# Gated delta rule on one core: key and query products built once per token block and kept in SBUF, and an output projection from seven block products

## The reference, cut to what matters

```python
q = l2norm(...) * GDN_DK ** -0.5; k = l2norm(...); v = ...     # 8 heads of 128
o_fwd = chunk_gated_delta(q, k, v, beta[:, :, 0], g[:, :, 0])
o_bwd = flip(chunk_gated_delta(flip(q), flip(k), flip(v), flip(beta[:, :, 1]), flip(g[:, :, 1])))
o = rmsnorm(o_fwd + o_bwd, norm_g) * silu(z)
return o.reshape(B, S, H * GDN_DV) @ w_out                     # [512, 1024] @ [1024, 1024]
...
L = where(strict, (kb @ k.T) * decay, 0);  T = inverse(eye + L)
u = T @ vb;  w = T @ (kb * exp(gc));  a_intra = (q @ k.T) * decay
v_new = u - w @ state;  o = (q * exp(gc)) @ state + a_intra @ v_new
state = state * g_last + kg.T @ v_new
```

## Time and profile before

| | us |
|---|---|
| runs | 1690.05, 1692.55, 1693.95; median 1692.55 |
| the profiled execution | 1698.45 |
| its span | 1696.7 |
| TensorE busy | 1596.5 |
| GDN periods 0 to 4 | 921.2 to about 1106.5 |
| output projection | 1106.5 to 1164.4 |

### The profile page before, as it was taken

One profiled execution on the slowest core, in us unless ns is written; L12 is line 12 of the kernel. 1 busy time (PEld: TensorE's weight loads), 2 busy tenths in 40 slices (PEclk: granted clock), 3 DMA queues, 4 the chain that ended last, 5 costly groups with the idle time before them and its releaser, 6 DMA issues.

```text
span 1696.7 us, 21245 instructions
## 1 busy us (share of the span) xinstructions
PE 1596.5 (94%) x8966; PEld 823.3 (49%) x8966; DVE 648.9 (38%) x1107; ACT 439.8 (26%) x972; POOL 183.1 (11%) x115
## 2 busy tenths in 40 slices
PE   7999899999989978899999999998999999999787
PEld 4464534343343324488875688855344433433233
DVE  3564411131210116789982566633111312102056
ACT  4232301101101003422125775542111010110043
POOL 2302000000000004352402211000000000000021
PEclk9999999999999999999999999999999999999999
DMA  8104699999999995012121110284899999999941
GB/s 289 72 14 185 267 422 424 396 427 430 425 426 425 428 424 202 0 50 101 50 100 50 27 27 2 101 347 198 369 426 391 428 426 428 424 428 428 426 184 50
DMA packets 54045, 454.56 MB, mean 268 GB/s; under 512 B 5187, under 2 KB 7519, under 8 KB 28991
## 3 DMA queue, kind: packets, MB, share of 16 engines
q1 hardware_dynamic: 53424, 452.90, 65.0%
q0 software_dynamic: 288, 0.22, 0.0%
q10 hardware_dynamic: 239, 0.09, 0.0%
HBM read 451.07 MB, written 2.13 MB: 267 GB/s over the span
## 4 chain that ended last, share of the span: by engine, by line
PE 70%; DMA 12%; DVE 11%; ACT 6%; issue 2%; DVEq 0%; ACTq 0%
PE banks L2116 31%; PE banks L1464 10%; DMA ring<-in_moe_w_down 8%; DVE misc L2540 4%; PE banks L2087 3%; PE banks L1745 3%; PE banks L1647 3%; PE banks L1999 3%; DMA ring<-in_moe_w_up 3%; PE banks L2149 3%; PE banks L1710 2%; PE banks L2177 2%; PE banks L1572 1%; PE banks L2125 1%; DVE misc L2538 1%
## 5 line engine op out<-in xcount | busy, mean ns | idle before, releaser
L2116 PE MATMUL banks<-ring,misc 128*64 128x512 f32 x1984 | 444.7, 599 | 10.7 <-DMA ring<-in_moe_w_up 5.7
L2116 PEld LDWEIGHTS banks<-ring,misc 128*64 128x64 f32 x1984 | 139.2, 138 | 286.8 <-issue 266.5
L2116 PE MATMUL banks<-ring,hid_t 128*64 128x512 f32 x960 | 216.1, 602 | 15.6 <-DMA ring<-in_moe_w_down 15.6
L2939 DVE TENSOR_TENSOR work<-work,banks 128x512 f32<-128x512 f32 x32 | 33.7, 1053 | 442.0 <-PE banks L2116 442.0
L1403 ACT ACTIVATE misc<-banks 32x512 f32<-32x512 f32 x64 | 37.5, 586 | 416.9 <-PE banks L2116 416.5
L2116 PEld LDWEIGHTS banks<-ring,hid_t 128*64 128x64 f32 x960 | 69.1, 138 | 153.0 <-issue 144.3
L2954 DVE COPY misc<-banks 32x512 f32<-32x512 f32 x64 | 44.2, 691 | 229.7 <-PE banks L2116 229.2
L798 POOL TENSOR_TENSOR ring<-ring 128x2048 f32<-128x2048 f32 x2 | 10.9, 5454 | 1098.2 <-DVE ring L2990 1098.2
L1464 PE MATMUL banks<-ring,xt 128*128 128x512 f32 (+1 forms) x280 | 118.9, 584 | 0.2
L2540 DVE SCALAR_TENSOR_TENSOR misc<-ring,conv_w,misc 128x512 f32<-128x512 f32 x96 | 93.8, 977 | 3.4
L1647 PE MATMUL banks<-ring 128*128 128x256 f32 x384 | 86.0, 380 | 0.0
(11 more groups left out here) (381 smaller groups left out, 1899.0 us busy)
## 6 DMA issues: line engine op xcount, KB each, us to landing
ring<-in_moe_w_gate SPq DMA_DIRECT2D x62, 2048.0 KB, 15.4
ring<-in_moe_w_up SPq DMA_DIRECT2D x62, 2048.0 KB, 18.3
ring<-in_moe_w_down SPq DMA_DIRECT2D x56, 2048.0 KB, 19.9
ring<-in_gdn_w_in SPq DMA_DIRECT2D x8, 2048.0 KB, 9.0
ring<-in_ple_w_gate SPq DMA_DIRECT2D x4, 2048.0 KB, 16.5
ring<-in_moe_w_down SPq DMA_DIRECT2D x6, 1024.0 KB, 23.6
ring<-in_mla_w_out SPq DMA_DIRECT2D x2, 2048.0 KB, 23.9
misc<-in_moe_w_down SPq DMA_DIRECT2D x2, 2048.0 KB, 15.7
```

The source lines that it names most:

```text
L2116: mm = pe.matmul(psum[64 * f:64 * f + 64, bank, :], tokens(4 * kh + k), row(k, f), start=(kh == 0 and k == 0), stop=(kh == 1 and k == 3))
```

## The change

Builds. `build_kk` runs for problems 0 and 2 only, `build_qk` likewise, into new stages `kb` and `qb` of 8 instead of 16 builds each, which ScalarE copies to SBUF (`keep_kk`, `keep_qk`). DVE reads the copies. They lie in `h`, which is written to DRAM before and read back after. Places: `keep_kk(0, a)` before the first exponentials; `kb` 0 to 3 as before; `qb` 0 to 3 at the end of period 0; `kb` 4 to 7 between the joins of period 1; `qb` 4 to 7 between those of period 2. The first product with the state (`new_state` or `with_state("qs")`, lane 0) moves to just after `dt5`.

Projection. Seven products of half the depth (`P1` to `P7`, two token blocks each) replace eight outputs of full depth. DVE makes two token sums and changes `a12`, GpSimd makes four weight sums and one token sum; DVE adds 28 times instead of 8.

```diff
+GO_PARTS = P1, P7, P2, P6, P5, P3, P4
+GO_ADDS = {P1: ((0, 0), (0, 1), (1, 0), (1, 1)), P7: ((1, 0), (1, 1)), P2: ((0, 0),), P6: ((0, 1), (1, 0), (1, 1)),
+           P5: ((0, 1), (1, 1)), P3: ((0, 1),), P4: ((1, 0),)}
...
-                if q + 1 < QS:
+                if q == 1:
                     for a in range(4):
-                        build_banks.add(core["kk"], 4 * q + 4 + a)
-                for a in range(4):
-                    build_banks.add(core["qk"], 4 * q + a)
+                        build_banks.add(core["kb"], 4 + a)
+                if q % 2 == 0:
+                    for a in range(4):
+                        build_banks.add(core["qb"], 2 * q + a)
...
                     for name in ("z5", "du5", "dt5", "z6"):
+                        if name == "z6" and p >= 2:
+                            apply_banks.add(core["st" if p % 2 == 0 else "qs"], 4 * (p // 2 - 1))
                         apply_banks.add(core[name], p - 1)
...
# SyncE
+                        if u == 2:
+                            sp.wait_ge(ple_added, 8)
+                            sp.dma_start(h_dram, flat_h).then_inc(x_in[3], 16)
...
                     sp.dma_start(gw_out[0], wo[:, :, 0:HALF]).then_inc(loaded[2], 16)
+                    for name in ("kk", "qk"):
+                        core[name].wait_read(sp, 15)
+                    sp.dma_start(flat_h, h_dram).then_inc(x_in[3], 16)
...
-                    frees[2] = s_go.full(8)
-                for m in ((0, 1, 2, 3, 6, 7, 4, 5), (1, 2, 3, 4, 6, 7, 0, 5))[l]:
+                    frees[2] = s_go.full(14)
+                    frees[7] = s_go.full(10)
+                for m in ((0, 1, 2, 3, 6, 7, 4, 5), (1, 3, 4, 6, 7, 0, 2, 5))[l]:
                     sp.wait_ge(*frees[slot_of(l, m)])
+                    if l == 1 and m == 2:
+                        sp.wait_ge(mo_weights, 8 + 5)
...
# GpSimd
+                wait_use(pool, "gdn_out0")
+                pool.wait_ge(gdn_out1_in, 16)
+                pool.wait_ge(*core["av"].full(12))
+                pool.tensor_tensor(go_t1, go_b12, go_b11, ALU.subtract).then_inc(mo_weights, 1)
+                pool.wait_ge(mo_weights, 8 + 1)
+                pool.tensor_tensor(go_b12, go_b22, go_b12, ALU.subtract).then_inc(mo_weights, 1)
+                s_gt.wait_read(pool, 3)
+                pool.wait_ge(*core["qs"].full(8))
+                pool.tensor_tensor(go_s3, go_a11, go_a21, ALU.subtract).then_inc(mo_weights, 1)
+                pool.wait_ge(*core["av"].full(16))
+                pool.tensor_tensor(go_t2, go_b22, go_t1, ALU.subtract).then_inc(mo_weights, 1)
+                pool.wait_ge(mo_weights, 8 + 4)
+                pool.wait_ge(*s_go.full(go_no(P2, 1) + 1))
+                pool.tensor_tensor(go_b21, go_b21, go_t2, ALU.subtract).then_inc(mo_weights, 1)
...
# ScalarE
+                def keep_kk(f, a):
+                    i, j = 4 * f + a, lane(2 * f, a)[3]
+                    src = bank(build_banks, "kb", i, P)
+                    if f == 0:
+                        act.wait_ge(x_in[3], 32)
+                    else:
+                        core["kk"].wait_read(act, 7)
+                    act.activation(c_kk[:, 4 * j:4 * j + 4, :], src, ACT.Copy).then_inc(core["kb"].freed(i)[0], 1)
...
+                for a in range(4):
+                    keep_kk(0, a)
                 for a in range(4):
                     exp_decay(0, a)
...
                         join64(prev)
+                        for a in range(2):
+                            if p == 1:
+                                keep_kk(1, a)
+                            if p == 2:
+                                keep_qk(1, a)
...
                         keep(apply_banks, "z6", prev, c_z6, 64)
+                        for a in range(2, 4):
+                            if p == 1:
+                                keep_kk(1, a)
+                            if p == 2:
+                                keep_qk(1, a)
...
                         gate_in(6)
                         gate_in(7)
+                    if p == 0:
+                        for a in range(4):
+                            keep_qk(p // 2, a)
...
# TensorE
                         level_z(p, 1)
+                    if p == 1:
+                        build_kk(2, 0)
+                    if p == 2:
+                        build_qk(2, 0)
                     if p:
                         z5(prev)
+                        if p == 1:
+                            build_kk(2, 1)
+                        if p == 2:
+                            build_qk(2, 1)
...
                         dt5(prev)
+                        if p == 1:
+                            build_kk(2, 2)
+                        if p == 2:
+                            build_qk(2, 2)
+                        if p >= 2:
+                            if p % 2 == 0:
+                                new_state(p - 2, 0)
+                            else:
+                                with_state("qs", p - 2, 0)
...
                         z6(prev)
+                        if p == 1:
+                            build_kk(2, 3)
+                        if p == 2:
+                            build_qk(2, 3)
...
+                project(P1, go_a11, go_b11, (0,))
                 core["av"].wait_read(pe, 15)
+                project(P1, go_a11, go_b11, (1,))
                 pe.wait_ge(gdn_out1_in, 16)
+                pe.wait_ge(mo_weights, 8 + 3)
+                project(P7, go_s3, go_b12, (0,))
                 turn_heads(1)
+                project(P7, go_s3, go_b12, (1,))
                 s_gt.wait_read(pe, KD - 1)
+                project(P2, go_a12, go_b21)
+                pe.wait_ge(mo_tokens, 8 + 2)
+                pe.wait_ge(mo_weights, 8 + 4)
+                project(P6, go_s2, go_t2)
+                project(P5, go_s1, go_t1)
+                pe.wait_ge(mo_tokens, 8 + 3)
+                project(P3, go_a12, go_b22)
+                pe.wait_ge(mo_weights, 8 + 5)
+                project(P4, go_a22, go_b21)
...
# DVE
-                    done("qk", i, dve.tensor_tensor(at, at, bank(build_banks, "qk", i, P), ALU.mult))
+                    done("qk", i, dve.tensor_tensor(at, at, c_qk[:, 4 * j:4 * j + 4, :], ALU.mult))
...
+                add_part(P1, 0)
+                add_part(P1, 1)
                 for k in (5, 7):
...
+                dve.tensor_tensor(go_s1, go_a21, go_a22, ALU.add).then_inc(mo_tokens, 1)
+                dve.tensor_tensor(go_s2, go_s1, go_a11, ALU.subtract).then_inc(mo_tokens, 1)
+                add_part(P7, 0)
+                add_part(P7, 1)
+                add_part(P2, 0)
+                add_part(P2, 1)
+                dve.tensor_tensor(go_a12, go_a12, go_s2, ALU.subtract).then_inc(mo_tokens, 1)
```

More of the change, by code:

```diff
@@ L516, in trunk_kernel @@
                     turn_banks.add(s_gt, k)
-                s_go = stage("gdn_proj", 2 * NJ, ["dve"], before=s_mo)
+                s_go = stage("gdn_proj", 14, ["dve"], before=s_mo)
+                banks.skip(2)
             L.s_xt = stage("ffn_xt", KD, AV, before=s_xt1 if l else s_xt0)
@@ L968, in norm_act @@
             i = norm_no[name]
-            f_last = 0 if name in ("ffn0", "mix1", "last") and j >= NT else 1
+            f_last = 0 if name in ("ffn0", "mix1", "ffn1", "last") and j >= NT else 1
             for f in (1 - f_last, f_last):
@@ L2626, in make_m @@
                         dve.wait_ge(*core["z6"].full(q - 1))
-                    done("kk", i, dve.scalar_tensor_tensor(out=c_m[q % 2][:, us, :], in0=bank(build_banks, "kk", i, P), scalar=-1.0,
+                    d, s, n, j = lane(q, a)
+                    dve.wait_ge(*core["kb"].freed(4 * (q // 2) + 2 * n + s))
+                    done("kk", i, dve.scalar_tensor_tensor(out=c_m[q % 2][:, us, :], in0=c_kk[:, 4 * j:4 * j + 4, :], scalar=-1.0,
                                                            in1=c_et[:, us, :], op0=ALU.mult, op1=ALU.mult))
@@ L2821, in gdn_dve, with add_part @@
                     gate_out(1, a)
+                def add_part(x, t):
+                    i = go_no(x, t)
+                    dve.wait_ge(*s_go.full(i + 1))
+                    if x != P1:
+                        dve.wait_ge(*s_go.freed(i - 2))
+                    for s, f in GO_ADDS[x]:
+                        hv = h_part(s, t, f)
+                        ins = dve.tensor_tensor(hv, hv, psum[:, banks.bank(s_go, i), :], ALU.add)
+                    ins.then_inc(s_go.freed(i)[0], 1)
+                dve.wait_ge(x_in[3], 48)
+                add_part(P1, 0)
+                add_part(P1, 1)
                 for k in (5, 7):
@@ L2825, in gdn_dve @@
                                       ALU.mult).then_inc(s_gt.freed(k)[0], 1)
-                for i in range(2 * NJ):
-                    j, f = i // 2, i % 2
-                    dve.wait_ge(*s_go.full(i + 1))
-                    hv = h[:, j, f * HALF:(f + 1) * HALF]
```

(23 more changed lines are left out.)

95 lines of the change are left out of this document (46 added, 49 removed).

## The result

The changed kernel takes 1696.68 us (median of 14 executions, 1691.21 to 1701.55), the kernel before, measured beside it, 1693.3 us (14, 1689.65 to 1697.41). The ratio is 1.0021, 95% interval 1.0011 to 1.003: about 3.4 us slower, where 8.5 us faster was forecast. The profiled execution of the changed kernel is 1695.93 us with a span of 1694.2. That is *shorter* than the profiled execution of before (1698.45), which was a long one of its kernel. So the first question was what in these two profiles is typical, and a second profile of before (1691.07 us, span 1689.3) answers it. It was expected that the stages of the core would agree within 1 us in the two; from the first turn to the turn of the heads they differ by 3.1 (180.0 and 176.9), by stretches at a low clock.

What follows compares the result with a forecast made beforehand. TensorE, with 70% of the chain, was taken as the main bound, with DVE and ScalarE setting parts of the periods. Stage terms summed to -10.7 us, the clock added 2.2: -8.5 from the 1692.55 median, 1684.0 us, range 1676 to 1692.

Steps and rivals of the forecast that it cites:

- Opening, +2.0: Ahead of the exponentials: ScalarE's key-product copies lie on the path, 0.6 + 3 x 0.49 = 2.07 us more.
- Period 0, -2.8: Period 0: four builds go, -3.56 us; 0.8 is given back for copies on ScalarE at its end.
- Period 1, +0.7: Period 1: copies ahead of spread_u +1.1, query builds gone at the end -1.6, DVE's second SBUF input +1.2 us.
- The port's term: Start of period 1: make_at, now with two SBUF inputs, waits for GpSimd's mask_decay, +1.2 us, between 0 and 2 x 1.24.
- Period 2, -4.0: Period 2: eight builds go, four come between the joins and keep the clock up; 4.0 us gained, between 2 and 7.
- Period 3, -2.0: Period 3: first query-state product earlier, so DVE's additions begin one earlier, -1.0; four query builds gone, -1.0 us.
- Period 4, +3.2: Period 4 to the heads' turn: z6 waits for join5, +1.0; DVE's gate instructions wait for GpSimd, +2.2 us.
- Projection, -7.8: Projection: 56 matmuls instead of 64, -6.9 us; a product hides the last head copies, -0.9; norms' tail as long.
- The clock, +2.2: Core: TensorE's new waits of 3 to 4 us bring one more low-clock fall on the path, +2.2 us, 0 to 6.6.
- Costed at nothing: The hidden state h written to DRAM and read back: hidden at both ends, 0 us, bounded by twice 8.8.
- the core gives nothing, or back what the projection brings: Rival, 0.23: TensorE waits wherever builds went, falling to 1.2 GHz each time; period 2 gives 2; -2.1 us, 1690.5.
- Slower: Rival, 0.08: ScalarE's queue bounds every period, sixteen copies cost +9.6 us, removed builds bring nothing; +6.2 us, 1698.8.

Runs made afterwards that it cites:

- after: The changed kernel as built and its profile: 1696.68 us median, 1.0021 to the kernel before; profiled execution 1695.93 us.
- the wide products: Changed kernel, second GpSimd weight difference behind the first four gate products, unread 512-column products in TensorE's waits of periods 0, 2, 3; about 2 us gained.
- the run with late transposes: Changed kernel, second GpSimd weight difference behind the first four gate products, unread transposes in wide waits of periods 2, 3, 4 alone; 1692.9 us, 1.0001.
- the run with the place alone: Changed kernel, second GpSimd weight difference behind the first four gate products, last four kept query products built at period 2's end; about 2 us gained.
- the split: Changed kernel with only the second of GpSimd's two weight differences waiting for the first four gate products; 1694.28 us, 0.9999 to the kernel before.
- core alone: Changed kernel with the old projection of 64 matmuls and the old expert load order, key products kept; 1699.57 us, 1.0047 to the kernel before.
- both gate variants: Changed kernel with both GpSimd weight differences behind the first four gate products (1701.87 us, 1.0059), or only the second (1694.28 us, 0.9999).
- the two with the place moved: The run with the place alone, and the same with the first state or query-state product behind the third small product again; no difference in time between them.

## Why the prediction was wrong, step by step

The sums of the forecast against what the two profiles and the experiments give:

- **Opening, +2.0:** right, +2.32 (15.36 against 13.04, in every profile of the new core).
- **Period 0, -2.8:** -1.5 in after, -2.9 at full clock (36.69 with the wide products). The mechanism was right; the fall of the clock behind the opening's wait, which the forecast saw coming, costs 1.4.
- **Period 1, +0.7:** +0.6 (36.79 against 36.18; 36.8 to 38.6 in the other runs of the new core with nothing unread ahead of it). Its first quarter is 2.4 longer, its last 1.6 shorter, as the terms say. The port's term was right in kind: the last two `make_at`, beside `mask_decay`, took 2.71 us instead of 1.25, and the two before them 1.74 instead of 1.25; no run takes the port apart from the copies.
- **Period 2, -4.0: this step failed.** It reads "If they keep it busy, the clock stays up and the first half costs what it did, with them in it." The period got 1.4 us longer against the first profile of before and 2.9 against the second. The gain in its second half was sized well: the last three quarters are 3.0 us shorter than undisturbed before (30.4 against 33.5). But the first costs 13.25 instead of 7.3. The premise was a window in which TensorE was busy 0.93 of 2.00 us, and that window holds most of the idle time of the whole first half. Here are its two quarters at full clock, second profile of before, then the first quarter with the builds in it at full clock (the run with late transposes):

```profile
993.89:1001.16 7.27, 5.98 (x231) 4.96 (x229) 4.23 (x8) 6.46 (x12) 0.00 (x0) 1.00 0.35 76
1001.16:1010.76 9.60, 9.60 (x176) 8.78 (x173) 6.80 (x13) 7.79 (x17) 0.00 (x0) 1.00 0.02 4
```

```profile
997.71:1009.90 12.19, 10.65 (x269) 9.53 (x270) 8.24 (x16) 8.86 (x17) 0.30 (x1) 1.00 0.27 69
```

 Idle are 1.29 us in the first quarter and none in the second. Into the first went three builds at 0.89 and a state product, 3.56 us; the fourth build went into the second. And even the 1.29 weren't filled: with the builds in it the quarter has 1.54 us of idle, as TensorE now waits 1.53 ahead of the first level products, where no build stands. At full clock the two quarters took 12.19 and 9.87 with the builds in them, 9.38 and 8.90 without, with about the same unread work in both: 3.8 us for four builds of 3.56, so their whole cost is on the path. Of the 6.0 us that the first quarter lost in after, the three builds and the state product are thus some 3.6, and the half clock about 2 (an estimate: 13.25 less the 12.19 at full clock without their 1.09 of transposes). The other premise, that they would keep the clock up, took the wrong end: the clock fell before they began, behind the wait that the removed query products left.
- **Period 3, -2.0:** failed likewise: its first quarter is 12.55 instead of 7.26. Of these 5.3 us 3.8 is half clock and 1.4 the query-state product moved ahead (8.92 against 7.56 without it). The same quarter at either clock, after, then the run with the place alone, which has no unread work:

```profile
1040.23:1052.78 12.55, 10.93 (x237) 9.72 (x238) 7.90 (x15) 7.86 (x15) 0.30 (x1) 0.52 0.01 3
```

```profile
1042.37:1051.08 8.71, 6.75 (x237) 5.97 (x238) 6.75 (x13) 8.08 (x16) 0.30 (x1) 1.00 0.02 5
```

 The gain from DVE starting one product earlier is there, 1.1 in the second quarter at full clock (8.49 against 9.58), but its cost on TensorE in the first was left out.
- **Period 4, +3.2:** the gate, +2.2, was right in kind and 0.7 too small (5.13 against 2.18; the split gave back 3.7 by the ratios). The third small product did wait for `join5` where the clock was up (1.48 us, in the run with late transposes), but in place of a wait of 1.43 for ScalarE, so the +1.0 isn't there; with the state product ahead the last quarter is even some 1 us shorter at the same mean clock (34.1 to 34.2 in three profiles against 35.1 and 35.2, all at 0.85).
- **Projection, -7.8:** -7.74 to the last product, exactly its eight groups and the hidden stall. "The norms' tail is as long" failed: 6.79 against 4.79. Before, one norm was left behind the last product; now four are ready only as its last parts end, and ScalarE and DVE take them one after the other:

```profile
1156.33 1.23 ACT L1030 ACTIVATE xn<-h,rstd 128x512 f32<-128x512 f32 x1 [2.46 <-DVE rstd L2364]
...
1159.66 1.23 ACT L1030 ACTIVATE xn<-h,rstd 128x512 f32<-128x512 f32 x1 [0.23 <-DVE rstd L2364]
...
1163.07 1.21 ACT L1030 ACTIVATE xn<-h,rstd 128x512 f32<-128x512 f32 x1 [0.30 <-DVE rstd L2364]
...
1166.46 1.22 ACT L1030 ACTIVATE xn<-h,rstd 128x512 f32<-128x512 f32 x1 [0.30 <-DVE rstd L2364]
```

 They follow each other every 3.4 us, and the last begins 4.3 us behind the last product's end (1162.20). Before it began 2.3 behind it (1166.72 against 1164.45), with the other three done.
- **The clock, +2.2:** too small in number, not in kind. The waits were forecast well: some 4, 3 and 4 us at the opening and at the ends of periods 1 and 2, where after has 4.48, 3.03 and 4.11. But only one fall was priced for all of them, and each of them brought one, also that ahead of the four builds that were to keep the clock up. After's core has about 24 us more at half clock than before's first profile, not 4. A fall costs most where small products stand back to back, as in the opening of period 3 (in that of period 2, with the builds out, 12.55 against 9.38), and the stretch goes on there; those products have waits of 0.5 to 1.6 us among them, but that these keep the clock low isn't shown, as the same quarter of before has such waits at full clock. One fall was priced at 2.2 us; the one of period 3 alone costs 3.8 in its first quarter.
- **Costed at nothing:** right. `h` came back 12.1 us after its issue at 1088.2, and the first addition to it began at 1121.5; on its way out it took 6.3 from 707.6.

The rival *the core gives nothing, or back what the projection brings*, 0.23, described what happened: TensorE waits wherever builds went and falls each time. Its -2.1 us was still too low by some 5; its price for period 2 was 2 us of gain. *Slower* had 0.08 and the wrong mechanism (ScalarE's copies everywhere). Copying on ScalarE was priced right where it could be read, in the opening; the slower kernel came from where TensorE's work was put.

Part of the error was hidden in the one profile that the sum used, whose core was itself disturbed: its own period 2, and period 3 up to the heads, are 1.5 and 1.7 us above those of the second. The first half of period 2 was taken to cost "what it did"; 1.5 us of that was a fall of the clock, at 1004. The slack counted in its second half was real: those two quarters are the same in both profiles.

## What to carry to other kernels

Work moved into a gap is free only up to the idle time of the whole stretch between two waits of the chain, so sum the idle time over that stretch, not over the emptiest window in it; here 3.56 us went into 1.29. Even that much is free only where the moved work can stand ahead of what TensorE waits for. Work taken away where another engine sets the pace leaves a wait, and here each one of 2.6 to 4.5 us at the head of a period was followed by half clock: with seven us of redundant products at the periods' ends this kernel was 3.6 us faster than without them. Before moving an engine's work beside another's on a shared path, look at everything of both that is still queued: the 3 us won by delaying GpSimd's two differences were lost three times over when they and the two sums behind them met DVE's next group.

## What the runs showed of the hardware

- DVE with two SBUF inputs against GpSimd: one wait for each DVE instruction, not one for the group. 1.14 us of work in four instructions took 10.21 beside three back-to-back GpSimd instructions: at each of GpSimd's ends one DVE instruction got through, and the next waited for the whole of GpSimd's next one. The forecast weighed waiting for one end (1.24 or 4.5 us). The Trainium skill, SBUF — State Buffer, section "Who interferes with whom", has the DVE instruction blocked, not slowed in proportion, and the runs agree with that: the four instructions took 3.07, 2.44, 4.59 and 0.34 us, the first three ending 0.15 behind GpSimd's.
- In the same kernel the low clock comes at other places from one execution to the next where waits are of 0.5 to 1.5 us: in before at 1004, 1045 and 1082 in one profile, at 964 and 1073 in the other. Behind the waits of 2.8 to 4.1 us that open periods 2 and 3 of after it came in all four profiles that have them and no unread work (after, core alone, both gate variants), behind one of 2.6 that opens period 2 in the two with the place moved and no unread work, and behind the 4.48 that opens period 0 in all eight that have it.
- In the two profiles with 34 small transposes ahead of the first turn of period 0, TensorE stood idle for 1.7 and 1.8 us in the middle of a run of matmuls in period 1, and the period took 43.0 and 42.3 us instead of 36.8; with four wide products in the same place (3.4 us of TensorE against 4.0) neither came. Why is open.
